# Unit-matrix products in TensorE's waits: a two-layer trunk on one core

## What is computed

```python
def run_layer(l, x, cond, shared, mix_p, ffn_p, ctx):
    m = jax.nn.silu(cond) @ ada_w + ada_b
    sh1, sc1, g1, sh2, sc2, g2 = jnp.split(m[:, None, :], 6, axis=-1)
    h = rms_norm(x, n1_g) * (1.0 + sc1) + sh1
    o, state = mixer_even(h, mix_p, ctx) if l % 2 == 0 else mixer_odd(h, mix_p, ctx)
    x = x + g1 * o
    h = rms_norm(x, n2_g) * (1.0 + sc2) + sh2
    f = swiglu(h, *ffn_p) if l % 2 == 0 else moe_swiglu(h, *ffn_p)
    return x + g2 * f, state
```

## Time and profile before

| | |
|---|---|
| time, median of 3 runs | 1369.52 us (1367.44 to 1371.34) |
| the profiled execution's own time | 1370.85 us |
| its span, first to last instruction | 1369.0 us |
| outside the span | 1.85 us |
| PE busy | 1245.4 us (91%) |
| DVE, ACT, POOL busy | 889.8, 758.2, 282.0 us |
| granted clock of TensorE, mean | 0.948 |
| bytes moved, mean rate | 277.67 MB, 203 GB/s |

### The profile page before, as it was taken

One profiled execution on the slowest core, in us unless ns is written; L12 is line 12 of the kernel. 1 busy time (PEld: TensorE's weight loads), 2 busy tenths in 40 slices (PEclk: granted clock), 3 DMA queues, 4 the chain that ended last, 5 costly groups with the idle time before them and its releaser, 6 DMA issues.

```text
span 1369.0 us, 19648 instructions
## 1 busy us (share of the span) xinstructions
PE 1245.4 (91%) x7681; PEld 1096.9 (80%) x7681; DVE 889.8 (65%) x1120; ACT 758.2 (55%) x1114; POOL 282.0 (21%) x227
## 2 busy tenths in 40 slices
PE   5986899899999998998969897999999999999895
PEld 2885566799989996996656695998989889989793
DVE  1537777553343344684674527887888889799686
ACT  3547775443323334433364326777777777877673
POOL 0057970200020003000041020030330312303103
PEclk9897899999999999998979798999999999999998
DMA  9661894343444345421417322999899899899882
GB/s 312 175 216 62 273 308 165 121 139 108 138 138 128 103 139 154 139 93 56 148 39 245 96 85 89 317 321 327 288 330 341 261 349 327 277 335 330 277 283 82
DMA packets 180248, 277.67 MB, mean 203 GB/s; under 512 B 8528, under 2 KB 107352, under 8 KB 180152
## 3 DMA queue, kind: packets, MB, share of 16 engines
q1 hardware_dynamic: 179064, 272.81, 60.4%
q0 software_dynamic: 1088, 3.56, 0.8%
HBM read 274.03 MB, written 2.31 MB: 202 GB/s over the span
## 4 chain that ended last, share of the span: by engine, by line
PE 71%; DVE 11%; issue 9%; ACT 4%; DMA 2%; POOL 2%; SPq 1%; DVEq 0%; ACTq 0%; POOLq 0%
PE psB L2096 5%; PE psB L2098 5%; PE psB L2097 5%; PE psB L1569 5%; PE psB L1571 5%; PE psB L1570 5%; PE psA L2096 4%; PE psA L2098 3%; PE psA L2097 3%; PE psA L1569 2%; PE psA L2047 2%; PE psA L1571 2%; PE psA L1570 2%; DVE Wl L2729 2%; PE psB L1824 2%
## 5 line engine op out<-in xcount | busy, mean ns | idle before, releaser
L2729 DVE TENSOR_TENSOR Wl<-raw,Wh 128x1408 fp32r<-128x1408 f32 (+2 forms) x144 | 246.9, 1738 | 57.1 <-ACT Wh L1469 56.2
L2160 DVE TENSOR_TENSOR Wl<-raw,Wh 128x2048 fp32r<-128x2048 f32 (+4 forms) x63 | 134.1, 2134 | 142.3 <-ACT Wh L1108 142.1
L1469 ACT CAST Wh<-raw 128x1408 fp32r<-128x1408 f32 (+2 forms) x144 | 197.1, 1376 | 26.7 <-PE psA L2098 14.3
L1108 ACT CAST Wh<-raw 128x2048 fp32r<-128x2048 f32 (+4 forms) x64 | 110.0, 1724 | 109.4 <-PE psB L1825 61.8
L2096 PE MATMUL psA<-Wh,hTh 128*128 128x352 f32 x360 | 118.3, 328 | 0.7 <-ACT hTl L1475 0.7
L2098 PE MATMUL psA<-Wh,hTl 128*128 128x352 f32 x360 | 116.4, 323 | 0.0
L2097 PE MATMUL psA<-Wl,hTh 128*128 128x352 f32 x360 | 116.0, 322 | 0.0
L1569 PE MATMUL psB<-Wh,hTh 128*128 128x256 f32 (+2 forms) x356 | 105.4, 296 | 7.4 <-DVE zq L2535 4.6
L1004 POOL TENSOR_TENSOR yc<-yc,work 128x414 f32<-128x414 f32 x90 | 101.2, 1148 | 47.3 <-ACT work L1207 43.2
L1570 PE MATMUL psB<-Wl,hTh 128*128 128x256 f32 (+2 forms) x356 | 104.4, 293 | 0.0
L1571 PE MATMUL psB<-Wh,hTl 128*128 128x256 f32 (+2 forms) x356 | 104.3, 293 | 0.0
(11 more groups left out here) (374 smaller groups left out, 3333.5 us busy)
## 6 DMA issues: line engine op xcount, KB each, us to landing
raw<-in_l_moe_w SPq DMA_DIRECT2D x108, 704.0 KB, 5.6
raw<-in_l_ada_w SPq DMA_DIRECT2D x40, 1024.0 KB, 5.4
raw<-in_l_ffn_w SPq DMA_DIRECT2D x28, 1024.0 KB, 5.3
raw<-in_l_moe_w SPq DMA_DIRECT2D x27, 768.0 KB, 6.8
gate_b<-in_l_moe_w SPq DMA_DIRECT2D x18, 768.0 KB, 7.1
gate_b<-in_l_moe_w SPq DMA_DIRECT2D x18, 704.0 KB, 5.8
raw_tail<-in_l_moe_w SPq DMA_DIRECT2D x18, 704.0 KB, 5.4
raw<-in_l_w_in SPq DMA_DIRECT2D x11, 1024.0 KB, 5.4
```

The source lines that it names most:

```text
L1108: act.copy(split_views(u)[1], split_views(u)[0]).then_inc(hi_ready, 1)
L1469: act.copy(half_of(Wh, h), raw_half(h)).then_inc(half_hi, 1)
L2160: dve.tensor_tensor(wl, w, wh.bitcast(F32), ALU.subtract).then_inc(lo_ready, 1)
L2729: dve.tensor_tensor(half_of(Wl, h), raw_half(h), half_of(Wh, h).bitcast(F32), ALU.subtract).then_inc(half_lo, 1)
```

## The change

A helper `hold(bank, n)` is new: PE multiplies `ident`, the 128x128 unit matrix, with 512 columns of the resident constants `cst`, both float32, n times into one bank, and nobody reads the result; the next product that is read from that bank begins it anew. It raises no semaphore. It is called at six kinds of place, 82 times 512 columns in all:

- in `turn`, ahead of the wait for `xn_ready`, 9, 11 and 7 times for the second, third and fourth norm; `free_t`, which stood behind that wait, now stands ahead of the holds;
- in the turns of the latent heads, ahead of the first group of the items, 10, 8, 5 and 3 times; here too `free_t` now stands ahead;
- in `attend(1)`, steps 0 to 5, 7 times, and in `attend(2)`, steps 18 to 23, 7 times, behind the scores and ahead of the wait for the exponentials;
- ahead of the second adaLN block in preparing attention 0, 8 times, behind a new wait for `spread_free`;
- at the end of `attend(2)`, 3 times ahead of the last `o_transpose` and 4 times behind it.

```diff
+HOLD_NORM = {1: 9, 2: 11, 3: 7}
+HOLD_TURN = (10, 8, 5, 3, 0, 0, 0)
+HOLD_STEPS = {1: {0: 2, 1: 1, 2: 1, 3: 1, 4: 1, 5: 1}, 2: {18: 1, 19: 1, 20: 2, 21: 1, 22: 1, 23: 1}}
+HOLD_PREP, HOLD_OUT = 8, 4
...
+            def hold(bank, n):
+
+                for _ in range(n):
+                    pe.matmul(bank[:, 0:512], ident, cst[:, 0:512], start=True, stop=True)
+
...
                 g = first["norm", l, w]["T"] + f
+                free_t(g)
                 if f == 0:
+                    hold(psT[g % 2], HOLD_NORM.get(norms[0], 0))
                     pe.wait_ge(xn_ready, norms[0] + 1)
-                free_t(g)
...
                         g = tgroup(a, s)
+                        if a > 0:
+                            hold(psX, HOLD_STEPS[a].get(s, 0))
                         pe.wait_ge(psA_free, f["A"] + s + 1)
                         free_t(g)
...
                 if a == 2:
+                    hold(psX, HOLD_OUT - 1)
                     o_transpose(a, NT - 1)
+                    hold(psX, HOLD_OUT)
...
                     else:
+                        pe.wait_ge(spread_free, EARLY_0)
+                        hold(psY, HOLD_PREP)
                         aside_spread(EARLY_0 + t - 1)
...
             for n in range(14):
+                free_t(g0 + n)
+                if n % 2 == 0:
+                    hold(psT[(g0 + n) % 2], HOLD_TURN[n // 2])
                 pe.wait_ge(*item_ready(TURNS2[n // 2]))
-                free_t(g0 + n)
```

## The result

The changed kernel takes **1381.98 us**, the median of four runs (1381.85 to 1383.24), against 1369.57 us for the kernel before in the same comparison (1367.44 to 1371.34). The ratio is 1.0095, with a 95% interval of 1.0079 to 1.0111: slower by 12.4 us. The profiled execution is one at the median; its span is 1380.1 us, 11.1 us longer than that of before.

What follows compares the result with a forecast made beforehand. PE was taken as the bound, paying for half-clock stretches at norms and attentions; 1.6 + 1.9 + 0 - 1.0 + 7.2 + 1.0 + 0 = +10.7 us gave 1381.5 us profiled, 1380 us median, range 1367 to 1388 us.

Steps and rivals of the forecast that it cites:

- The price of a hold: One 512-column float32 product on PE: 0.90 us at full clock, bounds 0.22 and 1.8 us; 82 holds are 74 us.
- Norms (0, 1) and (1, 0): 9 and 11 holds overrun PE's waits and the dense part gives nothing back: +1.6 and +1.9 us.
- Norm (1, 1): 7 holds delay the first transposes, but DVE sets the pace and the last block ends as before: 0 us.
- attention 1: 7 holds, two inside the first wait; full clock gains more than the rest adds: -1.0 us, bounds -6 and +4.5.
- preparing attention 0: 8 holds, 7.2 us, ahead of spread and block at full clock; POOL sets the pace: 0 us.
- The turns: 26 holds at the latent heads' turns; those behind freed banks delay ACT's copies and attention 2: +7.2 us, bounds 0 and +9.6.
- eight copies of 0.53 us remain, ACT's: Last link at the turns: after the last holds end at 723.9, ACT's copies end at 728.7 against 721.52.
- The end of attention 2: 14 holds, 12.6 us, plus PE's work at full clock make 25.2 us against 24.2 us before: +1.0 us.
- The clock stays at 1.00: Sign expected in the changed profile: full clock at the norms, the turns and the end of attention 2.
- Rival 1: Holds of 0.45 us or less fit their waits, keeping the clock up at no cost: -11.6 us, 1358 us; chance 0.14.
- Rival 2: The delay at the turns does not reach attention 2: sum +3.5 us, 1373 us; chance 0.14.
- Rival 3: Clock falls although PE multiplies, holds take up to 1.8 us: 1400 us or above; chance 0.04.

Runs made afterwards that it cites:

- short versions: Kernels whose holds have 256 columns instead of 512, or about half the count at full width; medians from 1355.59 to 1362.72 us.
- without turns: The changed kernel without the 26 holds at the turns of the latent heads, all other holds kept: 1373.03 us, ratio to before 1.0021.
- with turns alone: The changed kernel with only the 26 holds at the turns of the latent heads, all others removed: 1378.93 us, ratio to before 1.0074.

## Why the prediction was right

The forecast was 1380 us, and the median is 1381.98; the sum of +10.7 us for the profiled execution met one of +11.1 us. Point by point:

- **The price of a hold.** Taken at 0.90 us from `average`, measured 0.86 us; "starts 0.44 to 0.46 us apart" was a little too much, they are 0.429 us apart. The 2.98 us read for `average` hold a longer first step and the way to the next instruction besides the eight products; from one of its inner starts to the next it takes 0.35 us, which in proportion to the columns is 0.43 us. The Trainium skill (TensorE: Matmul & The Clock Gate, Back-to-back issue gap) gives 0.216 us as the isolated gap for 512 columns; the trace has that for split operands, 0.22 us, and twice that for each of a hold's two instructions. The Trainium skill (FP8 and Floating Point Precision, TensorE Precision Notes) has a true float32 product make four passes through the array: an estimate from both pages is 4 x 0.216 = 0.864 us, and the trace agrees within 1%.
- **Norms (0, 1) and (1, 0).** +1.6 and +1.9 us forecast, +1.16 and +1.41 us measured. The holds were 0.4 to 0.5 us shorter in a row than I took them, 7.72 us for nine and 9.44 us for eleven. That the dense part gives nothing back was right: between the two norms the timelines differ by less than 0.1 us.
- **Norm (1, 1)** at 0 was +0.23 us; **attention 1** at -1.0 was -1.16 us; **preparing attention 0** at 0 was -0.45 us, and the two kernels without holds there have -0.45 and -0.46 us, so it is not shown to come from the holds.
- **The turns.** +7.2 us forecast, +8.15 us measured. The chain was right link by link: the second pair of copies 4.43 us behind an idle ACT, three packets of holds each behind a freed bank. The mis-sized term is "eight copies of 0.53 us remain, ACT's". The last four pairs took 5.02 us from 724.04 to 729.06, where I had 4.24: ACT waits 0.25 us ahead of each of the last three pairs, since with two banks the transposes can't begin before a copy frees one. The last of the earlier trace rows has that wait already, 0.28 us.
- **The end of attention 2.** +1.0 us forecast, +0.49 us measured.
- **What I didn't foresee.** Attention 2 starts 2.77 us worse, with a stretch at 0.50 that before doesn't have. "The clock stays at 1.00" was checked for the places of the holds; I didn't ask what the clock does in the next wait without one. Holds at the first step remove it (0.00 us in the two kernels that have them, 1.17 to 2.78 us in the other ten). But the change is not shown to be the cause: the kernel with holds at the norms alone has no hold between norm (1, 0) and norm (1, 1), and it too is 1.57 us worse there. One profile of before was taken, and it may be the exception; that stays open. Against the 2.77 us stands -1.59 us at the start of the program, where the two kernels are the same. Neither was in the forecast, and they nearly cancel. That the sum is closer than its terms is thus in part luck.
- **Rival 1, a short hold.** Its price was wrong, and its mechanism right: with holds of 0.43 us the kernel gets faster, 1362.72 us, and with the turns' holds moved ahead 1356.71 us against the 1358 us forecast for it. "The turns 0" is the part that failed: holds behind the bank's wait cost 2.71 us even at half the price.
- **Rival 2, hidden turns**, falls by the kernels without turns and with turns alone, which put 8.95 and 9.1 us on them. **Rival 3**, a clock that falls although PE multiplies, falls by the strip and the rows at 1.00 where the holds stand; the one row at 0.50 with PE busy throughout, 733.20 to 740.00, has no hold in it.

## What to carry to other kernels

Work that only keeps an engine's clock up is worth something only as long as it ends inside the wait it fills, so size it by the measured price of an instruction of the same form, a plain float32 product being two instructions of 0.43 us each for 512 columns: here the same places gave +12 us with holds of the full length and -7 us with half of it, and -13 us with half of it and the turns' holds ahead of the bank's wait. Put it ahead of every wait of that place and in memory that needs no wait of its own; behind the wait that ends last it fills nothing and delays what was ready. And where another engine sets the pace, as at the turns of the latent heads, a higher clock is worth next to nothing, whatever it cost.

## What the runs showed of the hardware beyond that

The clock level of a stretch is not fixed by its instructions. The first 113 us are the same instructions in all thirteen kernels, and against before's profile the other twelve took 1.59 to 5.19 us less, counted from PE's first product. Attention 0 and the start of attention 2 differ in the same way between kernels whose instructions there are the same. Busy time by stretch of before, then of the kernel with holds at the turns alone:

```profile
0.00:108.00 108.00, 85.92 (x567) 74.24 (x568) 38.63 (x72) 54.08 (x93) 24.58 (x25) 0.92 0.74 223
```

```profile
0.00:108.00 108.00, 88.82 (x594) 76.41 (x595) 43.00 (x78) 57.79 (x100) 27.20 (x28) 0.98 0.74 223
```

At 0.98 instead of 0.92 the second has got 27 matmul instructions further by the same time. What decides it between executions stayed open; no kernel was run for it. It is also why single profiles of these kernels are compared here by stretches and not by spans, and why differences of 2 or 3 us between the short versions can't be told from their medians.
